# Page loads ahead of the mask, and one threshold search for blocks 4 to 7, in a hybrid decoder layer

## The chip, the cores and the metric

The kernel runs on one core of a Trainium2 chip. The metric is the device time of one execution in microseconds (us); lower is better. Engine names are those of the profile: PE (TensorE, with PEld for its weight loads), DVE (VectorE), ACT (ScalarE), POOL (GpSimd) and SP (SyncE, which here only issues transfers). An engine name with a q (SPq, DVEq) is that engine's sequencer.

## What is computed

One layer of a hybrid decoder for 1024 prompt tokens and, with the same weights, 64 sample tokens (8 sequences of 8, each with a cache of 4096 keys in 32 pages):

```python
x += 0.5 * swiglu(rms_norm(x), w1)
z  = rms_norm(x) @ w_in
#    attention: 8 query heads, 2 kv heads, dim 64, rotary; a token indexer picks the keys:
score = sum_h w[t,h] * relu(q_idx[t,h] . k_idx[s])
keep the 256 admissible keys of the largest score, softmax attention over these alone
#    short gated convolution, width 3: y = B * conv(C * h)
x += concat(attn, conv) @ w_out
x += 0.5 * swiglu(rms_norm(x), w2)
x += sigmoid(rms_norm(x) @ w_ple_gate) * (p @ w_ple_proj)
y  = rms_norm(x)
```

## The kernel before

**Tokens and products.** Tokens lie in columns, features in partitions. Group 0 has 576 columns, the 64 sample tokens and the prompt's blocks 0 to 3 (a block is 128 tokens), in two chunks of 288 (c0, c1). Group 1 is chunk c2 of 512 columns, blocks 4 to 7. A weight tile is 128 x 1024 in fp32. It is loaded raw (`load`, L603 to L610), ACT writes its rounded part (`w_hi`, `d_hi`, L834) and POOL the rest (`w_lo`, `d_lo`, L734), and each product is three matrix passes, hi by hi, lo by hi, hi by lo (L1442 to L1444). There are two raw buffers: a load waits until POOL has written the lo part two loads back, so SP, which issues the loads in order, sets the pace when it is held up.

**The order.** Class `Plan` writes one list of events (`order`, from L231), and each engine walks that list and does its own part of each event. The main line is a list of products, cut into parts. `weave(first, side, a, b)` hangs groups of side events on the places ("spots") between those parts, evenly from spot a to spot b. So an engine that is late with one event is late with all that the list has behind it, and a wait in one engine's program holds everything behind it on that engine.

**The stages**, in time: the norm of group 0 (`sq`, `sums`, `spread`, `scale`); SwiGLU 1 for group 0, with the gathering of indexer pages; the in-projection with the indexer's scores; SwiGLU 1 and the down products of c2, into which the sample tokens' search for their threshold is woven; the attention of the sample tokens and then of blocks 0 to 3, woven into the same products; `mix` and the out-projection of group 0; the in-projection of group 1; SwiGLU 2, into which the searches and the attention of blocks 4 to 7 are woven; out-projection, SwiGLU 2 of c2, embedding, final norm.

**Threshold search.** The 256th largest score of a row is found bit by bit. One iteration for two blocks (`bt`, `threshold_bit`, L1245 to L1259) is on DVE alone: a count per block of the scores at or above the candidate (L1242), a drain, a small operation per block (L1255), a drain, another per block (L1258), a drain. 32 iterations give the threshold. `places_left` (event `room`, L1264) and `choose` (event `bties`, L1274 to L1282) then settle equal scores and turn the score into a mask. Search A is for blocks 2 and 3, B1 for 4 and 5, B2 for 6 and 7. B1 has 8 iterations in the in-projection of group 1 and 24 in SwiGLU 2 ahead of the attention of block 4. B2's 32 iterations hang on the attention units of blocks 4 and 5,. The sample tokens have a like search of 32 bits over 2056 keys (`st`, L1284 to L1304), 12 in the in-projection and 20 behind it, then three events for ties (`sties`, L1308 to L1336), the last of which writes the mask `smask` (L1333) and lets go of semaphore `smask_ready`.

**Sample attention.** Behind the mask come: `sample_queries` on POOL (L766 to L778), the loads of pages of keys and values on SP (`kv_load`, L680 to L692; event kl), the split of the keys into `K_hi` on ACT (L993) and `kv_kr` on POOL (L784; event ks), the products of keys and queries on PE (event kq; L1442 to L1444 with `qs_hi`), the mask product (L1682) and the evacuation on DVE (`Sa`, L1384), then softmax, transposes and the product with the values (L1711). Buffers: 3 for keys, 8 for values.

```python
def kv_load(k):
    if k == 0:
        sp.wait_ge(smask_ready, 1)
```

Before every fourth kv_load, SP reads 16 page numbers from the table into registers (`page_numbers`, L613): one load and, for each number, a check of its bounds.

**Norm and mix.** `scale` multiplies x by the spread reciprocal (L1075), `spread` is a diagonal (L1069) times ones on PE (L1549). `mix` makes the hi and lo parts of the concatenated attention and convolution of a group: ACT writes four tiles of conv and then four of attn in two operations (L1020, L1021), POOL the lo part of conv (L788), DVE that of attn (L1425), and the out-projection waits for both.

Of the kernel before, what the change touches and what calls it, by code (L numbers as in the profile page):

```python
# [6 lines left out]
fp16 = mybir.dt.float16  # L7
# [36 lines left out]
SEARCH = {"A": (2, 3), "B1": (4, 5), "B2": (6, 7)}  # L44
EARLY = 8
# [50 lines left out]
class Plan:  # L96
# [134 lines left out]
    def order(self):  # L231
        squares = lambda k, c: [[("sq", k, c, m)] for m in range(KT)]
        flat = lambda groups: [e for g in groups for e in g]
        ev = [("begin",)] + flat(squares(0, 0)) + [("weights",)] + self.norm(0, 0) + flat(squares(0, 1)) + self.norm(0, 1)

        first = self.two_chunks(0, range(FT))
        first = weave(first, [[("ga", i)] for i in range(NB * PAGES // 2)], 1, 140)
# [13 lines left out]
        side += [[("st", j)] for j in range(12)]  # L251
# [3 lines left out]
        search = [[("st", j)] for j in range(12, 32)] + [[("sties", i)] for i in range(3)] + [[("qs",)]]  # L255
        groups = self.samples()
        for j in range(32):
            groups[6 + 2 * j].append(("bt", "A", j))
# [4 lines left out]
        first = weave(first, groups + units + [[], [("mix", 0)], [("back", 0)]], 51, -3)  # L263
        ev += weave(first, search, 2, 50)
# [6 lines left out]
        side += [[("bt", "B1", j)] for j in range(EARLY // 2)] + [[("vtr", 1)]] + [[("bt", "B1", j)] for j in range(EARLY // 2, EARLY)]  # L271
# [23 lines left out]
        ev += first[:end] + [("sums", 4, 0)] + first[end:end + 1] + [("spread", 4, 0)] + first[end + 1:]  # L295
# [3 lines left out]
    def with_weights(self, events):  # L299
# [9 lines left out]
        for e in events:  # L309
            if e[0] == "weights":  # L310
                for w in range(RING):
                    split(("w", w), "w", w)
# [77 lines left out]
def program(nc, t_in, t_out, x_spill, idx_flat):  # L390
# [5 lines left out]
    with ctx:  # L396
# [22 lines left out]
        small, small_i = at("small", [128, 64], f32, 5824), at("small_i", [128, 9], i32, 6080)  # L419
        carry = small[:, 0:8].rearrange("p (a b) -> p a b", b=2)  # L420
        mxr, nb, rs, ri = [small[:, 8 + 2 * j:10 + 2 * j] for j in range(4)]
        mx2, cnt, reached, room = small[:, 24:28].rearrange("p (a b) -> p a b", b=2), small[:, 28:36], small[:, 36:38], small[:, 38:40]
# [5 lines left out]
        cand, drop = [small_i[:, 2 * j:2 * j + 2] for j in range(2)]  # L428
# [169 lines left out]
        def _(sp):  # L598
# [81 lines left out]
            def kv_load(k):  # L680
                if k == 0:
                    sp.wait_ge(smask_ready, 1)
# [1129 lines left out]
```

## Time and profile before

| | us |
|---|---|
| median of 3 runs | 2928.32 |
| lowest and highest of them | 2918.21, 2932.49 |
| the profiled execution | 2924.44 |
| its span in the trace | 2922.7 |
| PE busy | 2615.3 (89% of the span) |
| DVE busy | 1313.0 (45%) |
| POOL busy | 1009.9 (35%) |
| ACT busy | 1001.1 (34%) |

The granted TensorE clock averages 0.943 of full speed over the profiled execution. Busy shares are averages over stages that have different limits; so the stages have to be read one by one. Drains and other sequencer work are not counted as busy.

### The profile page before, as it was taken

What the parts mean: (1) busy time and instruction counts of PE and PEld (TensorE: products, weight loads), DVE (VectorE), ACT (ScalarE), POOL (GpSimd) and SP (SyncE); (2) the same over time, 40 slices, a digit from 0 to 9 for tenths busy, and PEclk for the clock granted to TensorE, in tenths of its full rate; (3) what the DMA queues carried; (4) which work ended last, traced back from release to release, by engine and by line L of the source; (5) the groups of instructions that cost most, each with busy time, mean ns of one, the idle gap of its engine ahead of it and who ended that gap; (6) DMA issues with size and microseconds to landing.
All of it is one profiled execution on the core that took longest, in us unless ns stands there. A gap on an engine that the chain in (4) does not pass through costs nothing.

```text
span 2922.7 us, 41456 instructions
## 1 busy us (share of the span) xinstructions
PE 2615.3 (89%) x15166; PEld 2282.7 (78%) x15166; DVE 1313.0 (45%) x3135; ACT 1001.1 (34%) x1625; POOL 1009.9 (35%) x521
## 2 busy tenths in 40 slices
PE   4999998998868888889898976888999999999997
PEld 4999997778646767777786676777889898778786
DVE  3223224438753333443365687766333232332344
ACT  3222223631213333335435311443444233332332
POOL 4333333232343333332244223212213344454440
PEclk9999998999878888899999988998999999999998
DMA  4333324221224343311222212111112223233212
GB/s 147 98 95 100 107 92 140 93 106 63 96 79 124 103 136 116 119 57 49 77 101 75 70 61 73 44 44 44 44 44 87 80 72 115 87 108 96 92 63 73
DMA packets 157038, 253.40 MB, mean 87 GB/s; under 512 B 15010, under 2 KB 101283, under 8 KB 156835
## 3 DMA queue, kind: packets, MB, share of 16 engines
q1 hardware_dynamic: 154144, 247.02, 26.5%
q10 hardware_dynamic: 2690, 3.72, 0.4%
q8 instruction: 121, 1.98, 0.3%
q14 instruction: 83, 0.67, 0.1%
HBM read 240.34 MB, written 18.73 MB: 89 GB/s over the span
## 4 chain that ended last, share of the span: by engine, by line
PE 69%; DVE 14%; ACT 4%; issue 4%; POOL 3%; DVEq 2%; DMA 1%; SPq 1%; ACTq 0%
PE ps L1442 21%; PE ps L1443 19%; PE ps L1444 19%; PE ps L1655 2%; PE ps L1711 2%; DVE hits L1242 1%; POOL w_lo L734 1%; DVE s_hits L1292 1%; DVE hits_late L1242 1%; PE ps L1641 1%; DVE ps L1092 1%; POOL d_lo L734 1%; PE ps L1577 1%; DVE ha_lo L1094 1%; SPq L613 1%
## 5 line engine op out<-in xcount | busy, mean ns | idle before, releaser
L734 POOL TENSOR_TENSOR w_lo<-raw,w_hi 128x1024 fp32r<-128x1024 f32 x250 | 602.5, 2412 | 1058.7 <-ACT w_hi L834 1058.1
L1442 PE MATMUL ps<-xna_hi,w_hi 128*128 128x288 f32 x2000 | 612.3, 306 | 29.6 <-DVE convf_a L1146 7.8
L1443 PE MATMUL ps<-xna_lo,w_hi 128*128 128x288 f32 x2000 | 600.7, 300 | 0.0
L1444 PE MATMUL ps<-xna_hi,w_lo 128*128 128x288 f32 x2000 | 599.8, 300 | 0.0
L1442 PEld LDWEIGHTS ps<-xna_hi,w_hi 128*128 128x128 f32 x2000 | 387.6, 194 | 44.6 <-issue 22.8
L1442 PE MATMUL ps<-xnb_hi,w_hi 128*128 128x512 f32 x1000 | 412.8, 413 | 0.3 <-DVE hb_lo L1094 0.3
L734 POOL TENSOR_TENSOR d_lo<-raw,d_hi 128x1024 fp32r<-128x1024 f32 x90 | 218.4, 2446 | 544.6 <-ACT d_hi L834 544.6
L1443 PE MATMUL ps<-xnb_lo,w_hi 128*128 128x512 f32 x1000 | 400.6, 401 | 0.0
L1444 PE MATMUL ps<-xnb_hi,w_lo 128*128 128x512 f32 x1000 | 400.2, 400 | 0.0
L1443 PEld LDWEIGHTS ps<-xna_lo,w_hi 128*128 128x128 f32 x2000 | 387.3, 194 | 0.2
L1444 PEld LDWEIGHTS ps<-xna_hi,w_lo 128*128 128x128 f32 x2000 | 386.5, 193 | 0.0
L834 ACT ACTIVATE w_hi<-raw 128x1024 fp32r<-128x1024 f32 x250 | 263.6, 1055 | 193.0 <-PE ps L1444 106.1
L1442 PE MATMUL ps<-ha_hi,d_hi 128*128 128x288 f32 x704 | 216.2, 307 | 32.5 <-DVE xa L1183 28.8
L1442 PEld LDWEIGHTS ps<-xnb_hi,w_hi 128*128 128x128 f32 x1000 | 194.6, 195 | 46.1 <-issue 8.3
L1444 PEld LDWEIGHTS ps<-xnb_hi,w_lo 128*128 128x128 f32 x1000 | 194.3, 194 | 42.8
L1443 PEld LDWEIGHTS ps<-xnb_lo,w_hi 128*128 128x128 f32 x1000 | 194.8, 195 | 36.4
L1443 PE MATMUL ps<-ha_lo,d_hi 128*128 128x288 f32 x704 | 208.8, 297 | 0.0
L1444 PE MATMUL ps<-ha_hi,d_lo 128*128 128x288 f32 x704 | 208.4, 296 | 0.0
L834 ACT ACTIVATE d_hi<-raw 128x1024 fp32r<-128x1024 f32 x90 | 90.9, 1052 | 342.4 <-PE ps L1444 313.5
L1183 DVE SCALAR_TENSOR_TENSOR xa<-ps,xa 128x288 f32<-128x288 f32 x352 | 156.5, 455 | 109.7 <-PE ps L1444 109.4
L1183 DVE SCALAR_TENSOR_TENSOR xb<-ps,xb 128x512 f32<-128x512 f32 x176 | 121.6, 691 | 164.8 <-PE ps L1444 164.3
L1092 DVE TENSOR_TENSOR ps<-silu_a,ps 128x288 f32<-128x288 f32 x88 | 40.6, 462 | 287.0 <-PE ps L1444 274.8
(291 smaller groups left out, 4126.8 us busy)
## 6 DMA issues: line engine op xcount, KB each, us to landing
raw<-in_w_gu SPq DMA_DIRECT2D x176, 512.0 KB, 3.5
raw<-in_w_d SPq DMA_DIRECT2D x88, 512.0 KB, 3.5
raw<-in_w_ring SPq DMA_DIRECT2D x74, 512.0 KB, 3.4
pages<-in_vk_pages SPq DMA_DIRECT2D x256, 128.0 KB, 2.7
idx_flat<-in_idx_pages SPq DMA_DIRECT2D x256, 32.0 KB, 2.1
idxp<-idx_flat SPq DMA_DIRECT2D x8, 1024.0 KB, 7.6
x_spill<-xa SPq DMA_DIRECT2D x1, 2304.0 KB, 8.9
xa<-x_spill SPq DMA_DIRECT2D x4, 576.0 KB, 5.9
```

Of the source, the lines that this page charges most:

```text
L613: return nc.values_load_multi_w_load_instructions(ptab[0:1, first:first + k], engines=(mybir.EngineType.SP,), min_val=0, max_val=NPOOL - 1)[1]
L734: g_.tensor_tensor(lo[slot][:, :, :], raw[l % 2][:, :, :], hi[slot][:, :, :].bitcast(f32), ALU.subtract).then_inc(lo_done, 1)
L834: A(hi[slot][:, :, :], raw[l % 2][:, :, :], ACT.Copy).then_inc(hi_done, 1)
L1092: v.tensor_tensor(z, silu[g][:, own(c)], z, ALU.mult).then_inc(hmul_done, 1)
L1094: v.tensor_tensor(h_lo[g][h_at(c, j % 2)], z, h_hi[g][h_at(c, j % 2)].bitcast(f32), ALU.subtract).then_inc(h_ready, 1)
L1183: v.scalar_tensor_tensor(out=x[g][:, m, own(c)], in0=ps[:, 3 + (i - 1) % 2, 0:CH[c][1]], scalar=0.5, in1=x[g][:, m, own(c)], op0=ALU.mult, ...
L1242: v.tensor_scalar(hit[b][:, :], sc(b), level[:, i:i + 1], None, op, ALU.add, accum_out=reached[:, i:i + 1])
L1442: mm(out, shi, mhi, start=first, stop=False)
L1443: mm(out, shi, mlo, start=False, stop=False)
L1444: return mm(out, slo, mhi, start=False, stop=last)
L1655: mm(ps[rows, 7, c0:c0 + 128], V[:, j, rows], PT[g][r % 2][:, j, :], start=j == 0, stop=j == b)
L1711: last = mm(ps[:, 7, 64 * b:64 * b + 64], kv_v[(4 * ch + i) % V_RING][:, b, 128 * j:128 * j + 128], PTs[s][:, j, 64 * b:64 * b + 64], star ...
```

## The change

1. **Start.** The squares of the second chunk are woven into the norm of the first. Weight tiles 0 and 1 are split ahead of that norm as before, tiles 2 and 3 behind it. Product 0, on c0, starts ahead of the norm of c1.
2. **Sample search.** 10 of its 32 bits are in the in-projection, where 12 were; the other 22 and the ties are woven over spots 2 to 54 (2 to 50 before).
3. **Page loads and queries.** The first three kv_loads hang on the search's groups 2, 4 and 6 behind the in-projection, the first split of keys and `sample_queries` on its group 10. Their wait for the mask is replaced by a wait for the last product of the in-projection. For this, the key buffers `kv_kr`, `Sa`, the mask's and search's scratch lie elsewhere. The sample attention and blocks 0 to 3 go over spots 55 to -2 (51 to -3 before).
4. **Page numbers.** The check of bounds at run time is left out (`page_numbers`).
5. **Search B.** Blocks 4 to 7 have one search, 32 iterations of four counts, 8 of them in the in-projection of group 1 and 24 ahead of the attention of block 4. `bties` 5, 6 and 7 hang on the attention units 5, 10 and 15.
6. **Mix** goes tile by tile: ACT writes an attn tile and a conv tile in turn, DVE and POOL follow tile by tile, and the out-projection waits per tile.
7. **End.** `spread` of the last norm's c0 is behind the last embedding product, not one part ahead of it.

```diff
-SEARCH = {"A": (2, 3), "B1": (4, 5), "B2": (6, 7)}
+SEARCH = {"A": (2, 3), "B": (4, 5, 6, 7)}
...
-        ev = [("begin",)] + flat(squares(0, 0)) + [("weights",)] + self.norm(0, 0) + flat(squares(0, 1)) + self.norm(0, 1)
+        scales = lambda k, c, ms: [("scale", k, c, m) for m in ms]
+        second = flat(squares(0, 1))
+        ev = [("begin",)] + flat(squares(0, 0)) + [("weights", 0), ("sums", 0, 0)] + second[:4] + [("spread", 0, 0)]
+        ev += scales(0, 0, range(4)) + second[4:] + scales(0, 0, range(4, KT)) + [("weights", 1)]
...
+        ev += first[:1] + [("sums", 0, 1)] + first[1:2] + [("spread", 0, 1)] + scales(0, 1, range(KT))
...
-        side += [[("st", j)] for j in range(12)]
+        side += [[("st", j)] for j in range(10)]
...
-        search = [[("st", j)] for j in range(12, 32)] + [[("sties", i)] for i in range(3)] + [[("qs",)]]
+        search = [[("st", j)] for j in range(10, 32)] + [[("sties", i)] for i in range(3)]
         groups = self.samples()
+        for i in range(K_RING):
+            search[2 + 2 * i] += groups[i]
+        search[10] += [("qs",)] + groups[K_RING]
+        groups = groups[K_RING + 1:]
...
-        first = weave(first, groups + units + [[], [("mix", 0)], [("back", 0)]], 51, -3)
-        ev += weave(first, search, 2, 50)
+        first = weave(first, groups + units + [[], [("mix", 0)], [("back", 0)]], 55, -2)
+        ev += weave(first, search, 2, 54)
...
-        side = [[("bt", "B1", j)] for j in range(EARLY, 32)] + [[("room", "B1")]] + [[("bties", b)] for b in SEARCH["B1"]]
-        late = [[("bt", "B2", j)] for j in range(32)] + [[("room", "B2"), ("bties", 6)]] + [[("bties", 7)]]
-        for i, g in enumerate(units):
-            side.append((late[i] if i < len(late) else []) + g)
+        side = [[("bt", "B", j)] for j in range(EARLY, 32)] + [[("room", "B")]] + [[("bties", 4)]]
+        for b in (5, 6, 7):
+            units[5 * (b - 4)].append(("bties", b))
+        side += units
...
-        ev += first[:end] + [("sums", 4, 0)] + first[end:end + 1] + [("spread", 4, 0)] + first[end + 1:]
+        ev += first[:end] + [("sums", 4, 0)] + first[end:] + [("spread", 4, 0)]
...
-                                                                min_val=0, max_val=NPOOL - 1)[1]
+                                                                min_val=0, max_val=NPOOL - 1,
+                                                                skip_runtime_bounds_check_because="a page table holds pages of the pool")[1]
...
                 if k == 0:
-                    sp.wait_ge(smask_ready, 1)
+                    sp.wait_ge(prod_done, last_in[0] + 1)
...
-                pool.wait_ge(mix_hi, 2 * g + 1)
-                g_.tensor_tensor(xn_lo[g][:, 4:8, :], convf[g][:, :, :], xn_hi[g][:, 4:8, :].bitcast(f32), ALU.subtract).then_inc(mixc_ready, 1)
+                for j in range(4):
+                    pool.wait_ge(mix_hi, 8 * g + 2 * j + 2)
+                    g_.tensor_tensor(xn_lo[g][:, 4 + j, :], convf[g][:, j, :], xn_hi[g][:, 4 + j, :].bitcast(f32), ALU.subtract).then_inc(mixc_ready, 1)
...
-                A(xn_hi[g][:, 4:8, :], convf[g][:, :, :], ACT.Copy).then_inc(mix_hi, 1)
-                A(xn_hi[g][:, 0:4, :], attn[g][:, :, :], ACT.Copy).then_inc(mix_hi, 1)
+                for j in range(4):
+                    A(xn_hi[g][:, j, :], attn[g][:, j, :], ACT.Copy).then_inc(mix_hi, 1)
+                    A(xn_hi[g][:, 4 + j, :], convf[g][:, j, :], ACT.Copy).then_inc(mix_hi, 1)
...
-                for i in range(2):
+                for i in range(len(blocks)):
                     v.tensor_scalar(drop[:, i:i + 1], reached[:, i:i + 1], TOPK - 0.5, float(2 ** (31 - j)) if j else -1.0, ALU.is_lt, ALU.mult)
```

**Order of DVE at the end of the search, ahead of the first attention of block 4.** Scores 131 to 134 are those of blocks 4 to 7; L1102, L1104 and L1193 of the new file are the old L1092, L1094 and L1183 (work on the main products). Before:

```order
L1242 TENSOR_SCALAR hits_late,small<-score_131,small_i 128x640
L1242 TENSOR_SCALAR hits_late,small<-score_132,small_i 128x768
L1264 TENSOR_SCALAR small<-small 128x2
L1092 TENSOR_TENSOR ps<-silu_a,ps 128x288
L1094 TENSOR_TENSOR ha_lo<-ps,ha_hi 128x288
L1183 SCALAR_TENSOR_TENSOR xa<-ps,xa 128x288 x8
L1274 TENSOR_SCALAR equal_b<-score_131,small_i 128x640
```

In the changed kernel, the same place:

```order
L1252 TENSOR_SCALAR hits_late,small<-score_131,small_i 128x640
L1252 TENSOR_SCALAR hits_late,small<-score_132,small_i 128x768
L1252 TENSOR_SCALAR hits_late,small<-score_133,small_i 128x896
L1252 TENSOR_SCALAR hits_late,small<-score_134,small_i 128x1024
L1274 TENSOR_SCALAR small<-small 128x4
L1284 TENSOR_SCALAR equal_b<-score_131,small_i 128x640
```

The two larger counts now stand in every iteration ahead of the attention; before, they stood behind it, between attention units of blocks 4 and 5.

**Order of POOL around the sample queries.** Before (L767 to L778 are `sample_queries`):

```order
L734 TENSOR_TENSOR d_lo_76<-raw_64,d_hi_74 128x1024
L767 MEMSET qs_f 128x768
L773 COPY qs_f<-attn_a 64x4x8 x16
L776 CAST qs_hi<-qs_f 128x768
L778 TENSOR_TENSOR qs_lo<-qs_f,qs_hi 128x768
L734 TENSOR_TENSOR w_lo_71<-raw_63,w_hi_67 128x1024
L734 TENSOR_TENSOR w_lo_72<-raw_64,w_hi_68 128x1024
L784 TENSOR_TENSOR kv_kr_192<-pages,K_hi_123 128x512
L784 TENSOR_TENSOR kv_kr_193<-pages,K_hi_124 128x512
```

In the changed kernel:

```order
L744 TENSOR_TENSOR w_lo_71<-raw_63,w_hi_67 128x1024
L777 MEMSET qs_f 128x768
L783 COPY qs_f<-attn_a 64x4x8 x16
L786 CAST qs_hi<-qs_f 128x768
L788 TENSOR_TENSOR qs_lo<-qs_f,qs_hi 128x768
L794 TENSOR_TENSOR kv_kr_194<-pages,K_hi_123 128x512
L744 TENSOR_TENSOR w_lo_72<-raw_64,w_hi_68 128x1024
```

The queries and the first split of keys are a dozen weight splits ahead of the second split of keys, that is, in the midst of the search.

**Order of SP around the first page loads.** Before (L613 reads the page numbers, L692 is a page load):

```order
L610 DMA raw_63<-in_w_gu 128x1024
L613 TENSOR_LOAD ptab
L613 ISA x32
L692 ISA
L692 DMA pages<-in_vk_pages 128x2x128
```

In the changed kernel:

```order
L619 DMA raw_64<-in_w_d 128x1024
L622 TENSOR_LOAD ptab
L702 ISA
L702 DMA pages<-in_vk_pages 128x2x128
```

The 32 instructions of the bounds check are gone, and the first page load stands some 50 weight-load rows earlier in SP's program.

## Rows read from the trace of the kernel before

**Rows 1.** The page, busy time of each engine.

```profile
PE 2615.3 (89%) x15166; PEld 2282.7 (78%) x15166; DVE 1313.0 (45%) x3135; ACT 1001.1 (34%) x1625; POOL 1009.9 (35%) x521
```

**Rows 2.** Windows: stretch, us, PE, PEld, DVE, ACT, POOL busy, PEclk, DMA share, GB/s.

```profile
640.00:851.00 211.00, 179.55 (x897) 155.02 (x896) 175.48 (x327) 46.11 (x60) 89.07 (x44) 0.91 0.23 75
851.00:872.00 21.00, 1.43 (x7) 1.06 (x6) 0.05 (x1) 2.55 (x5) 10.18 (x15) 0.63 0.27 82
872.00:1294.00 422.00, 363.55 (x1847) 301.61 (x1846) 155.67 (x559) 141.74 (x232) 145.10 (x91) 0.85 0.38 111
1294.00:1447.00 153.00, 143.67 (x737) 107.12 (x736) 61.67 (x201) 79.98 (x167) 40.30 (x20) 0.99 0.16 52
1690.00:1812.00 122.00, 93.52 (x646) 91.61 (x644) 95.05 (x260) 22.25 (x34) 36.49 (x15) 0.90 0.21 66
1812.00:2050.00 238.00, 200.53 (x1293) 179.16 (x1293) 166.89 (x482) 96.07 (x156) 50.19 (x23) 0.91 0.14 45
2050.00:2245.00 195.00, 190.81 (x1342) 170.60 (x1342) 62.19 (x191) 92.33 (x140) 44.10 (x19) 1.00 0.15 49
```

**Rows 3.** Timeline of the start, ACT and PE: start, us, engine, instruction [idle before].

```profile
20.34 1.06 ACT L834 ACTIVATE w_hi<-raw 128x1024 fp32r<-128x1024 f32 x1 [5.73 <-DMA raw<-in_w_gu]
22.99 1.28 ACT L860 ACT_TABLE_LOAD   x1
41.75 0.59 PE L1442 MATMUL ps<-xna_hi,w_hi 128*128 128x288 f32 x1
```

**Rows 4.** Timeline behind the mask: DVE, POOL, SP, ACT, PE.

```profile
847.85 0.69 DVE L1333 TENSOR_SCALAR smask<-above 128x2056 bf16<-128x2056 bf16 x1
853.83 1.80 POOL L778 TENSOR_TENSOR qs_lo<-qs_f,qs_hi 128x768 fp32r<-128x768 f32 x1
863.61 4.69 SPq L692 DMA_DIRECT2D pages<-in_vk_pages  x6
868.86 0.63 ACT L993 ACTIVATE K_hi<-pages 128x512 fp32r<-128x512 f32 x1 [16.16 <-DMA pages<-in_vk_pages]
870.97 0.55 PE L1442 MATMUL ps<-K_hi,qs_hi 128*128 128x256 f32 x1 [19.57 <-POOL kv_kr L784]
```

**Rows 5.** Line 613 on SP, 858 to 864 us: count, ns min/median/max, first and last start.

```profile
L613 SPq FUSED_REGOPS  x16: 147/147/165, 859.4 to 863.2; - x16
```

**Rows 6.** Waits of PE: 872 to 1294 us, then 1812 to 2050: us, times, longest.

```profile
PE ps L1442 <- POOL kv_kr L784: 44.7, 15, 4.7
...
PE ps L1442 <- DVE small L1347: 21.8, 11, 6.6
```

**Rows 7.** Timeline of DVE: an iteration of B1, then one of B2.

```profile
1673.95 0.88 DVE L1242 TENSOR_SCALAR_CACHE_REDUCE hits_early<-score,small_i 128x640 bf16<-128x640 f32 x1 [0.16 <-issue]
1676.57 0.88 DVE L1242 TENSOR_SCALAR_CACHE_REDUCE hits_early<-score,small_i 128x640 bf16<-128x640 f32 x1
...
1814.12 1.15 DVE L1242 TENSOR_SCALAR_CACHE_REDUCE hits<-score,small_i 128x896 bf16<-128x896 f32 x1
1816.55 0.21 DVE L1255 TENSOR_SCALAR small_i<-small 128x1 int32<-128x1 f32 x2
1816.84 0.34 DVE L1258 TENSOR_SCALAR small_i<-small_i 128x1 int32<-128x1 int32 x2
```

**Rows 8.** Timeline of DVE: the ties of block 5, first and last operation.

```profile
1801.55 0.61 DVE L1274 TENSOR_SCALAR equal_b<-score,small_i 128x768 bf16<-128x768 f32 x1
1810.15 0.56 DVE L1282 TENSOR_SCALAR score<-score 128x768 f32<-128x768 f32 x1
```

**Rows 9.** Timeline of the mix of group 0: POOL, DVE, PE.

```profile
1445.88 5.07 POOL L788 TENSOR_TENSOR xna_lo<-convf_a,xna_hi 128x2304 fp32r<-128x2304 f32 x1
1447.49 5.87 DVE L1425 TENSOR_TENSOR xna_lo<-attn_a,xna_hi 128x2304 fp32r<-128x2304 f32 x1 [7.98 <-ACT xna_hi L1021]
1453.62 0.58 PE L1442 MATMUL ps<-xna_hi,w_hi 128*128 128x288 f32 x1 [6.34 <-DVE xna_lo L1425]
```

**Rows 10.** Timeline of DVE near the end: the last norm's scales.

```profile
2909.61 3.48 DVE L1075 SCALAR_TENSOR_TENSOR xna_f<-xa,consts,ps 128x288 f32<-128x288 f32 x8
```

More of the change, by code:

```diff
@@ L310, in with_weights @@
             if e[0] == "weights":
-                for w in range(RING):
+                for w in (2 * e[1], 2 * e[1] + 1):
                     split(("w", w), "w", w)
@@ L427, in program @@
         s_w, s_f = small[:, 28:32], small[:, 32:36]
-        cand, drop = [small_i[:, 2 * j:2 * j + 2] for j in range(2)]
-        s_cand, s_with_bit, s_drop = [small_i[:, 6 + j:7 + j] for j in range(3)]
+        room = {"A": small[:, 40:42], "B": small[:, 28:32]}
+        cand, drop = [small_i[:, 4 * j:4 * j + 4] for j in range(2)]
+        s_cand, s_with_bit, s_drop = [small_i[:, 8 + j:9 + j] for j in range(3)]
         raw = [at(f"raw{s}", [128, KT, 128], f32, 38912 + 4096 * s) for s in range(2)]
@@ L499, in program @@
         inv = [at("inv_a", [128, 128], f32, XNA + 16384), at("inv_b", [128, 128], f32, XNB + 24576)]
-        above = at("above", [128, HW], bf16, XNA + 17152)
-        cum = at("cum", [128, HW], fp16, XNA + 21280)
-        Sa = [at(f"Sa{s}", [128, 1024 + NS], f32, XNA + 16384 + 4352 * s) for s in range(2)]
+        above = at("above", [128, HW], bf16, XNA + 6144)
+        cum = at("cum", [128, HW], fp16, XNA + 10272)
+        Sa = [at(f"Sa{s}", [128, 1024 + NS * s], f32, FREE + 4096 * s) for s in range(2)]
         qs_hi, qs_lo, qs_f = [at(name, [128, 4, 192], dt, XNA + o) for name, dt, o in (("qs_hi", f32r, 25088), ("qs_lo", f32r, 28160), ("qs_f", f32, 28160))]
@@ L1277, in choose @@
                 dve.drain()
-                v.scalar_tensor_tensor(out=ti, in0=ti, scalar=room[:, i:i + 1], in1=e, op0=ALU.is_gt, op1=ALU.mult)
+                v.scalar_tensor_tensor(out=ti, in0=ti, scalar=room[name][:, i:i + 1], in1=e, op0=ALU.is_gt, op1=ALU.mult)
                 dve.drain()
@@ L1423, in mix @@
             def mix(g):
-                dve.wait_ge(mix_hi, 2 * g + 2)
-                v.tensor_tensor(xn_lo[g][:, 0:4, :], attn[g][:, :, :], xn_hi[g][:, 0:4, :].bitcast(f32), ALU.subtract).then_inc(mixa_ready, 1)
+                for j in range(4):
+                    dve.wait_ge(mix_hi, 8 * g + 2 * j + 1)
+                    v.tensor_tensor(xn_lo[g][:, j, :], attn[g][:, j, :], xn_hi[g][:, j, :].bitcast(f32), ALU.subtract).then_inc(mixa_ready, 1)
             does = {"begin": begin, "sq": square, "sums": sums, "spread": spread, "scale": scale, "p": product, "d": add,
@@ L1496, in product @@
                         pe.wait_ge(lo_done, plan.pos["w", w] + 1)
-                    if kind == "out" and key[0] == 0:
-                        pe.wait_ge(mixa_ready, g + 1)
-                        pe.wait_ge(mixc_ready, g + 1)
                 k = {"gate": 2 * key[0], "up": 2 * key[0], "in": 1, "out": None, "pg": 3}[kind]
@@ L1505, in product @@
                         normed(k, c, kt)
+                    elif (g, kt) not in mixed:
+                        mixed.add((g, kt))
+                        pe.wait_ge(*((mixa_ready, 4 * g + kt + 1) if kt < 4 else (mixc_ready, 4 * g + kt - 3)))
                     last = split_mm(out, hi[slot][:, kt, :], lo[slot][:, kt, :], xn_hi[g][:, kt, own(c)], xn_lo[g][:, kt, own(c)], kt == 0, kt == KT - 1)
```

52 lines of the change are left out of this document (25 added, 27 removed).

## The prediction

> **What bounds the kernel now.** I read the page's busy times first, then a table of windows by stage, then the timelines of the gaps. PE is busy for 2615 us of 2923 [rows 1], so over the whole program the products bound it, and only the stretches in which PE idles or has a low clock can give anything. The windows [rows 2] show three kinds. From 2050 to 2245 PE is busy 190.8 of 195 us at full clock: nothing to gain. From 640 to 851 (sample search) and from 1690 to 1812 (search B1) DVE sets the pace: its busy time is 175 of 211 and 95 of 122 us, and drains and dispatch, which are not counted, fill the rest. From 872 to 1294 (sample attention) no engine is full, but PE idles 58 us in short waits, and the granted clock is 0.85, which is another 63 us (15% of 422) below full speed. Between them stands a hole: from 851 to 872 PE works 1.4 us.
>
> **Start.** PE's first product pass is at 41.75 [rows 3]. ACT must split tiles 2 and 3 before it may compute the first norm, and idles 5.7 us for their load: from about 14.6, where tiles 0 and 1 are done, to 22.99, where the table load for the norm starts, 8.4 us go by. The change lets the norm go first, and runs product 0 on c0 before c1 is normed. Upper bound of the gain: 8.4 plus part of one chunk's product (24 passes, which start 0.24 us apart in the same timeline, 5.8 us), limited by weights that then are needed sooner: 12. Lower: 6, if the fourth tile's split becomes the next wait. **I take -10.**
>
> **Mask to first sample product.** The mask is written at 847.85 to 848.54. Only then POOL builds the queries, until 855.6, SP reads page numbers and issues page loads from 863.61 on, ACT splits the first keys at 868.86, and PE starts at 870.97 after 19.57 us of waiting [rows 4]. Afterwards all of this lies in the search. POOL's 6.7 us there (848.9 to 855.6) cost nothing, since POOL is busy 89 of 211 us and PE waits for DVE [rows 2]. On SP three kv_loads of four page DMAs at 4.69/6 = 0.78 us, 3.1 us each, plus the first read of numbers, are moved past weight loads; the DVE-bound search covers them. If that cover were gone, each could hold a weight load by 3 to 4 us, 12 in all. What stays: two more iterations and the ties behind the in-projection end the search some 3.5 us later, the mask product and its evacuation take about 2, and PE has about one more product part to do meanwhile. First sample product at 854 to 855: **-16.5**, between -12 and -20.
>
> **Sample attention.** SP reads 16 numbers before every fourth kv_load, and checks each: 16 checks start between 859.4 and 863.2, 0.253 us apart [rows 5], so 4.05 us of each read goes. PE waits 44.7 us in 15 waits for the keys' lo part, the longest 4.7 [rows 6]. But POOL, which makes it, is also in the queue behind weight splits, and only about five of these waits, some 15 us together, lie where SP was reading numbers. The others stay. From these I take 11 us. The first three key blocks are loaded ahead, so the wait and the low clock of the first 28 us go too: the first passes at 870.97 take 0.55 us against 0.41 of the next [rows 4], at the 0.63 clock of the hole [rows 2]; I put 8. And 3 for clock regained behind shorter waits. **-22**; nothing if POOL's queue is what sets these waits, -35 if nearly all go. The units are also spread a little tighter (117 groups on 99 spots, where 121 were on 102): nothing.
>
> After a wait the trace shows the clock low: 0.63 in the hole, 0.85 over the waits of this stage, 1.00 where PE hardly idles [rows 2]. The Trainium skill, page "TensorE: Matmul & The Clock Gate", section "HAM oscillation — how this bites in real kernels", says that a wait that comes back in every round of a loop drops TensorE to half clock each round, so that it costs more than its own length. The rows agree; by this rule the five shorter waits would give more than the 3 us that I add, which is the way of the second rival below.
>
> **Page reads elsewhere.** The gathers of the first stage get shorter by about 2 us per read of 8; loads run ahead there. Nothing.
>
> **Mix.** DVE's lo part of attn takes 5.87 us, 1447.49 to 1453.36, while POOL's of conv runs until 1450.95; it seems to run in its last 2.4 us alone. PE idles 6.34 us for it, to 1453.62 [rows 9]. By tiles the out-projection starts at about 1447 and follows the tiles, whose last comes at 1451 to 1453.5. Its own 5.8 us of passes then overlap. **-4**, between -2 and -7. The Trainium skill, page "SBUF — State Buffer", section "Who interferes with whom", says that a DVE operation with two SBUF inputs and a GpSimd operation exclude each other for a whole instruction. The row looks just like this; by the rule smaller operations do not overlap either, and the gain is 5 and not 6.
>
> **Search B.** An iteration of B1 takes 1676.57 - 1673.95 = 2.62 us. The two larger counts with their drain take 1816.55 - 1814.12 = 2.43, 2.27 without the drain, and two more of each small operation (0.21 and 0.34 for two, started 0.29 and some 0.43 apart) about 0.4 [rows 7]. So an iteration of four is 2.62 + 2.27 + 0.4 = 5.29, 2.67 more; 32 of them put 85.4 us on DVE ahead of the first attention unit of block 4. To this comes the larger `room`, 2.3. Off this path go the ties of block 5, 1801.55 to 1810.71, 9.2 us [rows 8], and the first four B2 iterations that DVE ran before the first logits, 12.6; and DVE has about 4 us of slack in the in-projection. 85.4 + 2.3 - 9.2 - 12.6 - 4 = 62; with a little for waits of PE behind longer iterations **+64**. None of this is covered: DVE is the bound there [rows 2], and PE's products wait behind it (its banks of PSUM are emptied by DVE).
>
> What comes back: from 1812 to 2050 DVE had 28 iterations of 3.15 us between its logits, and PE idled 37 us and lost 0.09 of 238, 21 us, to the clock [rows 2]; 21.8 of the idle were waits for logits evacuated late [rows 6]. Without the search the stretch should look like its neighbours. At the 98% of 2050 to 2245 it would give 45 us beyond what is counted above; at the 94% of 1294 to 1447 (blocks 2 and 3, no search) 35. The ties of blocks 5, 6 and 7 now stand in it (9, 6 and 7 us without logits), which costs about 5. **-30**; bounds -45 and, if the attention's own chain of logits, exponent and transposes sets these waits, -10. Search B in all: +34, from +19 to +54.
>
> **End.** The diagonal, spread and eight scales (3.48 us, [rows 10]) of the last norm come behind the last part instead of beside it: **+2**, from 0 to +3.
>
> **Sum.** -10 - 16.5 - 22 - 4 + 64 - 30 + 2 = -16.5 us. The profiled execution took 2924.4, 3.9 below the median, so it gives 2907.9 there and about **2911 us** against the median of 2928.3. About 0.5% (14.6 us) is what a measurement of this kernel can tell from no change: faster is below 2913.7, slower above 2942.9.
>
> **Rivals.**
> 1. *The search isn't paid back, slower.* Place: DVE, 1690 on. The other parts make -10 - 16.5 - 4 + 2 = -28.5, the search +64: +35.5 stands before sample attention and recovery, which together must give over 35.5 for any gain. If the short waits in the sample attention are POOL's queue (0 to -2) and the attention of blocks 4 to 7 is held by its own chain (-8), the kernel takes 2924.4 + 26 = 2950, or 2954 on the median's scale. For it: DVE is the only engine at its limit from 1690 to 1812, and every one of the 85 us lands there. Against it: the stretch from 2050 on shows what attention without a search does, at larger blocks. It decides from a recovery under about 16 us with no gain in the sample attention.
> 2. *Large gain.* Recovery 45, sample attention 35: 35.5 - 80 = -44.5, 2880, or 2884 against the median. For it: 98% and a full clock from 2050 on; the clock comes back with the idle. Against it: POOL's place in the chain of the keys, and the ties.
> 3. *The hole only shrinks.* The new loads don't do what they should: PE reaches the mask product early and now waits there for DVE, which has two more iterations and the evacuation, or weights are late behind the page loads. Mask to product -5, sample attention -12: the sum is +5, 2929.4, or 2933. For it: DVE, not the loads, sets when the mask comes, and it comes later. Against it: the chain from 848.5 to 871 has no work of DVE in it [rows 4].
>
> **Chances.** The forecast 0.42, its own range 2895 to 2927, of which some two thirds lie below 2913.7; rival 1 0.19; rival 2 0.21; rival 3 0.18, mostly within 0.5%. Faster: 0.28 + 0.21 = 0.49; same: 0.14 + 0.16 + 0.03 = 0.33; slower: 0.16 + 0.02 = 0.18. The range takes in most of rival 2 and half of rival 1: 2880 to 2950.
>
> **What would show it.** In the changed profile: first product pass at 30 to 33 us; PE's gap before the first pass on K_hi under 4 us, and L1384 within 3 us of the mask; no FUSED_REGOPS on the line of the page numbers, 11 us less of PE's waits for kv_kr, a clock over 0.87 in the sample attention; a first out-projection pass on the mixed input within 2 us of the last product; iterations of four counts every 5.3 us, the stretch from the first late one to the ties of block 4 about 62 us longer; PE busy 94% or more from there to the out-projection, and few waits for logits. I am wrong if iterations are shorter than 4.9 us, if DVE has other slack that hides them, or if the waits of PE in the attention stay as they were without the search on DVE.

## The result, and the profile after

The changed kernel takes **2934.91 us** (median of 20 runs, 2920.82 to 2941.59) against 2925.6 us for the kernel before (20 runs, 2918.21 to 2934.79): ratio 1.0026, 95% interval 1.0014 to 1.0038. That is slower by 0.26%, within the 0.5% that I called no change. I had forecast 2911, with a range of its own from 2895 to 2927, and a 0.33 chance of no change. The profiled execution took 2941.6 us and is the slowest of the 20, 6.7 above their median; keep that in mind with the offsets below, which come from this execution.

Windows of the changed kernel, by the same stages as [rows 2] (columns as there):

```profile
650.00:837.00 187.00, 164.25 (x795) 139.29 (x793) 147.27 (x299) 41.42 (x51) 78.98 (x49) 0.94 0.28 88
837.00:847.00 10.00, 1.03 (x5) 0.69 (x4) 8.88 (x6) 0.00 (x0) 8.15 (x3) 0.77 0.32 106
847.00:1250.00 403.00, 351.88 (x1821) 292.47 (x1821) 158.47 (x553) 140.09 (x231) 140.25 (x89) 0.87 0.39 114
1615.00:1668.00 53.00, 38.59 (x180) 32.06 (x178) 49.93 (x146) 9.62 (x11) 14.31 (x6) 0.88 0.17 50
1668.00:1833.00 165.00, 85.81 (x512) 83.55 (x513) 140.93 (x432) 17.70 (x28) 28.49 (x12) 0.72 0.13 42
1833.00:2060.00 227.00, 209.50 (x1398) 190.51 (x1397) 90.54 (x241) 99.29 (x158) 56.37 (x25) 0.94 0.16 52
2060.00:2258.00 198.00, 193.55 (x1363) 173.03 (x1362) 63.21 (x195) 94.27 (x145) 44.10 (x19) 1.00 0.15 48
```

The hole of 21 us is 10 now, the sample attention is at clock 0.87 and not 0.85. In their place stands the row from 1668 to 1833: 165 us in which PE is busy for half and its clock averages 0.72. Behind it (1833 on) PE is at 92%.

The two traces can be laid over each other, since PE runs the same 12312 passes on weights, numbered from 0, in the same order. This table, worked out from both traces, gives how much later (+) the changed kernel starts the same pass:

| pass number | where | changed minus before, us |
|---|---|---|
| 0 | first product | -18.8 |
| 400 to 3200 | SwiGLU 1, in-projection | -13.7 |
| 3600 | late in-projection | -18.7 |
| 4400 | in the sample search | -14.1 |
| 4800 | in the sample attention | -33.9 |
| 5600 | blocks 2, 3 | -40.8 |
| 6400 | in-projection of group 1 | -40.6 |
| 6800 | late joint search begun | -6.5 |
| 7200 | its end | +41.2 |
| 8000 | attention of group 1 | +22.9 |
| 9200 to 11200 | to the embedding | +10.7 to +12.2 |
| 12311 | last | +14.7 |

Everything ahead of search B gains 40 us; search B takes 82, and 29 come back behind it. Such offsets scatter from one execution to the next. Experiments 1, 3, 5 and 12 run the changed kernel's order up to pass 6400, and their offsets to the kernel before stand there at -52.0, -45.9, -41.4 and -41.3, where the changed kernel has -40.6.

The rows that answer to [rows 3], [rows 4], DVE, PE, in the changed kernel:

```profile
14.72 1.28 ACT L871 ACT_TABLE_LOAD   x1
...
22.91 0.58 PE L1453 MATMUL ps<-xna_hi,w_hi 128*128 128x288 f32 x1 [2.04 <-POOL xna_lo L750]
...
845.24 0.70 DVE L1343 TENSOR_SCALAR smask<-above 128x2056 bf16<-128x2056 bf16 x1
848.32 0.42 DVE L1394 TENSOR_SCALAR_CACHE_REDUCE Sa<-ps 128x256 f32<-128x256 f32 x1 [2.11 <-PE ps L1693]
...
846.34 0.55 PE L1453 MATMUL ps<-K_hi,qs_hi 128*128 128x256 f32 x1 [8.97 <-issue]
```

The table load is 8.3 us earlier, as said. The first sample product follows the mask at once: keys and queries are ready. But PE has waited 8.97 us for the mask, since its program waits for it ahead of the key products (L1675 of the new file) and not ahead of the mask product (L1693), which is the first to read it.

Two joint iterations that follow each other on DVE (answer to [rows 7]):

```profile
1750.04 0.87 DVE L1252 TENSOR_SCALAR_CACHE_REDUCE hits_late<-score,small_i 128x640 bf16<-128x640 f32 x1
...
1755.28 0.88 DVE L1252 TENSOR_SCALAR_CACHE_REDUCE hits_late<-score,small_i 128x640 bf16<-128x640 f32 x1
```

5.24 us, where I had 5.29. The unit price was right; the waits around it were not. Waits of DVE from the first joint iteration to the first logits (us, times, longest), of the changed kernel:

```profile
DVE xa L1193 <- PE ps L1455: 18.1, 24, 1.5
DVE ps L1102 <- PE ps L1455: 6.0, 1, 6.0
DVE ha_lo L1104 <- ACT ha_hi L895: 5.8, 10, 1.5
```

and of the kernel before, over its stretch from the first B1 iteration:

```profile
DVE xa L1183 <- PE ps L1444: 13.0, 24, 1.5
DVE ha_lo L1094 <- ACT ha_hi L884: 4.8, 10, 0.5
DVE ps L1092 <- PE ps L1444: 2.3, 2, 1.4
DVE tb L1151 <- PE ps L1444: 1.9, 2, 1.5
```

The sum of these waits went up by about 8 us (22.0 to 29.9), where I had counted 4 us of slack to be used up. Of the 29.9 us, 13.0 lie behind the last joint iteration, in the 23 us before the first logits.

### The profile page after: what moved, and what is told of

Same layout as the page of the kernel before. It is cut to its first block, busy times and chain, and to the rows that moved or that the text cites. A ratio compares the mean times of both kernels' runs of the same rounds, so it can differ in the third digit from the quotient of the medians.

```text
span 2939.8 us, 40350 instructions
## 1 busy us (share of the span) xinstructions
PE 2622.8 (89%) x15166; PEld 2290.8 (78%) x15166; DVE 1303.8 (44%) x3139; ACT 1001.0 (34%) x1637; POOL 1010.7 (34%) x527
## 4 chain that ended last, share of the span: by engine, by line
PE 71%; DVE 15%; ACT 4%; issue 3%; POOL 3%; DVEq 1%; DMA 1%; ACTq 0%; SPq 0%
PE ps L1453 21%; PE ps L1454 20%; PE ps L1455 20%; DVE hits_late L1252 3%; PE ps L1666 2%; PE ps L1722 2%; PE ps L1652 1%; POOL w_lo L744 1%; DVE s_hits L1302 1%; POOL d_lo L744 1%; DVE hits_early L1252 1%; DVE ps L1102 1%; PE ps L1588 1%; ACT w_hi L845 1%; DVE ha_lo L1104 1%
## 5 line engine op out<-in xcount | busy, mean ns | idle before, releaser
L1193 DVE SCALAR_TENSOR_TENSOR xa<-ps,xa 128x288 f32<-128x288 f32 x352 | 156.4, 455 | 117.6 <-PE ps L1455 117.4
L1453 PEld LDWEIGHTS ps<-ha_hi,d_hi 128*128 128x128 f32 x704 | 137.7, 196 | 85.4 <-DVE xa L1193 64.4
L1193 DVE SCALAR_TENSOR_TENSOR xb<-ps,xb 128x512 f32<-128x512 f32 x176 | 121.4, 691 | 173.9 <-PE ps L1455 173.4
```

The lines of the kernel that those rows point to most:

```text
L1193: v.scalar_tensor_tensor(out=x[g][:, m, own(c)], in0=ps[:, 3 + (i - 1) % 2, 0:CH[c][1]], scalar=0.5, in1=x[g][:, m, own(c)], op0=ALU.mult, ...
L1453: mm(out, shi, mhi, start=first, stop=False)
```

## The experiments

All were run in several rounds beside the kernel before on the same chip; experiments 1 to 4, 5 to 8 and 9 to 12 ran on three different chips. "Against the changed kernel" below is a difference of two such ratios, times 2926; each ratio is uncertain by about 0.0015 to 0.002, so such a difference by some 6 us, and by 8 between experiments 1 and 9.

**1. The change without the joint search.** Part 5 put back, all else as changed.

```diff
-SEARCH = {"A": (2, 3), "B": (4, 5, 6, 7)}
+SEARCH = {"A": (2, 3), "B1": (4, 5), "B2": (6, 7)}
...
+        late = [[("bt", "B2", j)] for j in range(32)] + [[("room", "B2"), ("bties", 6)]] + [[("bties", 7)]]
```

> The changed kernel with only its part 5 (one search for blocks 4 to 7) put back as before: B1 of 24 iterations ahead of the attention, B2 inside it. Theory (the joint search costs about 53 us net, which is what the offset between the two traces grows by from the in-projection of group 1 to the out-projection): 2935 - 53 = 2882 us, ratio to the kernel before about 0.985. Rival 1 (it costs the 34 us of the prediction, and the other parts gave less than forecast): 2901 us, ratio 0.992. Rival 2 (the search is neutral, the rest gave nothing): 2935.

2885.62 us, ratio 0.9858 (0.9839 to 0.9877). Against the changed kernel -49 us. The theory stands, its rivals fall. The offset of its passes to the kernel before is -52 us when group 1's in-projection starts, and stays at -50 to -54 to the embedding. The prediction had summed -52.5 for the parts ahead of that point (-10 - 16.5 - 22 - 4), but that the two agree is luck: this profiled execution is at the fast end of its runs, some 9 us below their median, so the median's share is nearer to -43, and the changed kernel's own trace has -40.6 there. From that point on the two traces differ by 54 us.

**2. The joint search alone.** Part 5 in the kernel before.

```diff
-SEARCH = {"A": (2, 3), "B1": (4, 5), "B2": (6, 7)}
+SEARCH = {"A": (2, 3), "B": (4, 5, 6, 7)}
```

> The kernel before with only part 5 of the change. Theory: 2926 + 53 = 2979 us, ratio 1.018. Rival 1 (34 us): 2960, ratio 1.012. If both this and the split search give 53 the parts add up; if this gives much less, the joint search hurts only in company of the other parts.

2970.22 us, ratio 1.0147 (1.0124 to 1.017): +43 us. In its trace the search adds 79 us and the attention gives 33 back. The loss is the joint search's own; 43 lies in the middle between 53 and 34, and by the two pairs the joint search costs 43 to 49 us, which are one number within the error.

**3. Eight iterations fewer.**

```diff
-        side = [[("bt", "B", j)] for j in range(EARLY, 32)] + [[("room", "B")]] + [[("bties", 4)]]
+        side = [[("bt", "B", j)] if j < 24 else [] for j in range(EARLY, 32)] + [[("room", "B")]] + [[("bties", 4)]]
```

> The changed kernel with the last 8 of the 24 late joint iterations left out (so the thresholds of blocks 4 to 7 lack their 8 lowest bits), their spots kept empty. If DVE alone sets the pace there, 8 x 5.29 = 42 us go: 2893. If, as I now suspect, DVE's waits for PE grow with the low clock of PE between the iterations (8.7 us more such waits in the changed trace over 24 + 8 iterations, where the forecast had 4 us less), an iteration is worth 5.7 to 6 us: 2888. If PE, not DVE, set the pace, under 30 us go: over 2905.

2896.53 us, ratio 0.9883 (0.9866 to 0.9901): 42 us below the changed kernel. By the offset of the passes only 34 of it lie in the search; 5 lie in stages ahead, which this edit does not touch, and so are scatter. Windows of the stretch with iterations, and of the empty one behind it:

```profile
1663.00:1769.00 106.00, 55.69 (x323) 54.21 (x324) 90.18 (x273) 11.57 (x18) 17.40 (x8) 0.71 0.11 36
1769.00:1795.00 26.00, 25.65 (x193) 25.42 (x193) 11.03 (x31) 6.25 (x10) 11.16 (x5) 1.00 0.39 123
```

Where the iterations are gone, PE is busy 25.65 of 26 us at full clock, and it, not DVE, sets the pace. Eight iterations of 5.24 us are 42 us; 34 came, and the rest is what PE needs for its own products there. My guess of 5.7 to 6 us an iteration is not borne out; nor is the rival in which PE sets the pace throughout (under 30 us).

**4. The check of page numbers put back** into the changed kernel.

```diff
-                                                                min_val=0, max_val=NPOOL - 1,
-                                                                skip_runtime_bounds_check_because="a page table holds pages of the pool")[1]
+                                                                min_val=0, max_val=NPOOL - 1)[1]
```

> The changed kernel with the run-time check of the page numbers put back (4.05 us more per read of 16 numbers, 16 reads). Theory (five or so waits of PE lie behind a read, and the clock falls with them): +14 us, 2949, ratio 1.008. Rival (POOL's queue of weight splits sets the waits for the keys' lo part, the reads are hidden): 0 to +3, 2935 to 2938. Third: the first read now stands inside the search, so nothing there.

2964.7 us, ratio 1.0127 (1.0108 to 1.0145): +30 us, twice the theory, and the two rivals (0 to +3, nothing) fall. The profiled pair differs by 21.8 us, and by the passes 20.5 of it arise between the first sample product and the out-projection. PE's waits of that stage, with the check,

```profile
PE ps L1452 <- POOL kv_kr L793: 52.5, 20, 5.1
```

and in the changed kernel,

```profile
PE ps L1453 <- POOL kv_kr L794: 42.8, 15, 4.7
```

are 10 us apart. The clock is 0.84, against 0.87 in the changed kernel:

```profile
849.00:1272.00 423.00, 359.99 (x1801) 297.47 (x1801) 154.78 (x551) 138.17 (x228) 139.57 (x88) 0.84 0.38 109
```

PE is busy for 8 us more than in the changed kernel's row (847 to 1250), on 20 fewer operations; that is the part of the clock.

**5. PE kept busy in the search.**

```diff
+            def warm(name, j):
+                if name == "B" and j >= EARLY:
+                    for _ in range(5):
+                        mm(ps[:, 6, 0:128], ones[:, :], ident[:, 0, :], start=True, stop=True)
```

> The changed kernel with five idle matrix products (ones times identity, 128 columns, into a PSUM bank that nobody reads, about 0.5 us each) on PE at each of the 24 late joint iterations. Theory: DVE's waits for PE in the search (18.1 + 7.6 + 5.8 us on the adds and the SwiGLU products, against 13.0 + 3.4 + 4.8 before) grow because PE comes out of each wait at half clock; with PE kept busy its clock stays up, these waits fall back by up to 10 us, and the kernel takes 2925 to 2930. Rival: they are the latency of a product that DVE has asked for late, whatever the clock; then 2935, or slower by as much as the idle products delay a real one (up to 2950).

2933.48 us, ratio 1.0015 (1.0002 to 1.0028): 3 us less than the changed kernel, within the error; the theory's 5 to 10 us did not come.

```profile
1668.00:1833.00 165.00, 104.87 (x737) 103.15 (x737) 142.10 (x435) 17.70 (x28) 28.42 (x12) 0.79 0.14 42
```

PE's clock rose from 0.72 to 0.79, DVE's waits on the additions fell from 18.1 to 15.8 us, and the search ended about as late as before (1 to 2 us). So 0.07 of clock gives back a small part of the waits. The experiment did not bring the clock to 1.00, so it doesn't exclude that the clock explains more of them. The rest is taken to be the time of a product part that PE can start only when DVE has emptied a bank; that was not tried by itself.

**6. Pages and queries behind the mask again.**

```diff
-        for i in range(K_RING):
-            search[2 + 2 * i] += groups[i]
-        search[10] += [("qs",)] + groups[K_RING]
-        groups = groups[K_RING + 1:]
...
-                    sp.wait_ge(prod_done, last_in[0] + 1)
+                    sp.wait_ge(smask_ready, 1)
...
-                pool.wait_ge(prod_done, last_in[0] + 1)
+                pool.wait_ge(smask_ready, 1)
```

> The changed kernel with its part 3 undone: sample queries, first page loads and first split of keys wait for the mask again and stand behind it (memory map and all else as changed). Theory: the hole of 21 us comes back in place of the 9 us that PE now waits for the mask, and the clock falls with it: +11 to +17, 2946 to 2952, ratio 1.0065 to 1.0085. Rival: the early loads hold up the weight loads in the search, or set back the key ring, so that they gain little: 2935 to 2940.

2946.69 us, ratio 1.0049 (1.0031 to 1.0066): +7 us, between the theory (+11 to +17) and the rival (0 to +5), and not to be told from either within the error. The first sample product starts at 858.8 and not 846.3, 12.5 us later, and PE waits 20.0 us there and not 9.0. But fewer products are done at that moment in the changed kernel (at pass 4800 the kernel of this run is even 9 us ahead, at pass 6000 9 us behind). The edit also puts 121 groups, not 117, on the same 99 spots, and the mask is written at 840.2 and not 845.2, since the search's last group hangs on an earlier spot. So part of the 7 us can be these, and the early loads are not weighed cleanly.

**7. Mix in its old form.**

```diff
-                for j in range(4):
-                    A(xn_hi[g][:, j, :], attn[g][:, j, :], ACT.Copy).then_inc(mix_hi, 1)
-                    A(xn_hi[g][:, 4 + j, :], convf[g][:, j, :], ACT.Copy).then_inc(mix_hi, 1)
+                A(xn_hi[g][:, 4:8, :], convf[g][:, :, :], ACT.Copy).then_inc(mix_hi, 1)
+                A(xn_hi[g][:, 0:4, :], attn[g][:, :, :], ACT.Copy).then_inc(mix_hi, 1)
...
```

> The changed kernel with mix in its old form (part 6 undone). Prediction on record: +4. Theory from the changed trace (the four DVE and four POOL operations alternate and take 9.4 us together where two long ones took 7.5; PE starts at once but waits for each tile): 0 to +2, 2935 to 2937. Rival: +6, 2941.

2937.33 us, ratio 1.0023 (1.001 to 1.0036): no difference. In the changed kernel:

```profile
1406.70 7.60 POOL L799 TENSOR_TENSOR xna_lo<-convf_a,xna_hi 128x576 fp32r<-128x576 f32 x4
...
1404.85 8.17 DVE L1436 TENSOR_TENSOR xna_lo<-attn_a,xna_hi 128x576 fp32r<-128x576 f32 x4 [3.13 <-ACT xna_hi L1030]
```

Four tiles each take 7.60 and 8.17 us side by side, 9.45 from the first start to the last end; the two long operations took 7.48 [rows 9]. They take turns: DVE's tiles start at 1404.85, 1407.27, 1409.19 and 1411.07, POOL's at 1406.70, 1408.61, 1410.49 and 1412.37. By the Trainium skill, page "SBUF — State Buffer", section "Who interferes with whom", such a pair excludes each other for a whole instruction. These rows agree.

PE does idle less at this place: 0.80 + 1.21 + 1.21 us in the changed kernel, 6.20 us in one wait with the old form. By the passes of the two traces the tiles bring the first mixed pass 6.4 us forward; 3.4 are left once the last tile is there, and 1.9 twenty passes later. The 1.5 us between are clock: at passes 5736 to 5741 PE is still at the low clock in the changed kernel, 0.43 us from one pass of 512 columns to the next, where with the old form it is 0.23. In the next in-projection 0.7 are left; where the rest went the record doesn't show, and such amounts are within the scatter.

**8. The check left out, alone.** The edit of experiment 4 the other way, in the kernel before. It takes out 512 checks, 256 in 16 reads of 16 numbers and 256 in 32 reads of 8 for the gathers.

> The kernel before with part 4 alone (no run-time check of page numbers). Theory (as when the check is put back into the changed kernel, +30 us): 2926 - 25 = 2901, and in the windows most of it between 872 and 1294 us, half as clock and half as idle. Rival: in the order before, the reads lie elsewhere; -14 us as predicted for the five waits and their clock, 2912. The waits for the keys' lo part alone can't tell, they sum to 43 to 46 us in all kernels but that with the check in the changed order (52.7).

2902.4 us, ratio 0.9912 (0.9896 to 0.9929): -26 us. The theory stands; its rival, the 14 us of the prediction, falls. By the passes 20 us of it lie in the hole and the sample attention (4 ahead of the first sample product, 16 behind it), and 4 between passes 100 and 200: the first read of numbers for the gathers had held up the weight loads behind it on SP, and a wait of PE of 2.9 us at 65 us is gone.

**9. Split searches, 12 bits, old end.** Experiment 1 with 12 bits of the sample search in the in-projection, and the last spread where it was.

```diff
-        side += [[("st", j)] for j in range(10)]
+        side += [[("st", j)] for j in range(12)]
...
-        search = [[("st", j)] for j in range(10, 32)] + [[("sties", i)] for i in range(3)]
+        search = [[("st", j)] for j in range(12, 32)] + [[("sties", i)] for i in range(3)]
...
-        ev += first[:end] + [("sums", 4, 0)] + first[end:] + [("spread", 4, 0)]
+        ev += first[:end] + [("sums", 4, 0)] + first[end:end + 1] + [("spread", 4, 0)] + first[end + 1:]
```

> The changed kernel with the searches of blocks 4 to 7 split as before, 12 and not 10 bits of the sample search in the in-projection, and the last norm's spread where it was. Against the run with the split searches alone (2885.6): the two bits cost 2 x 3.5 us of DVE in the search and gave 5 to 9 in the in-projection, so -2 to +3, and the end -2: 2880 to 2886. Rival: the search's place decides by more (the mask comes 7 us earlier and the K blocks are there): 2876.

**2876.18 us**, ratio 0.9824 (0.9804 to 0.9844), the fastest of the kernels that compute the whole layer: 10 us below experiment 1, where the error is about 8. It agrees with the rival's number, 2876. At pass 3600, late in the in-projection, its trace is 7 us later than that of experiment 1, and from the sample attention on 5 us earlier; the mask is there at 839.1 and not 842.9. The two profiled executions differ by 4 us only, so the trace bears out the sign, and less than the 10 us. The two bits moved out of the in-projection cost more than I gave them.

**10. The same, sample attention two spots later.**

```diff
-        first = weave(first, groups + units + [[], [("mix", 0)], [("back", 0)]], 55, -2)
+        first = weave(first, groups + units + [[], [("mix", 0)], [("back", 0)]], 57, -2)
```

> As the first run of this call, with the sample attention starting two spots later (57), so that PE has products to do in the 9 us that it waits for the mask. Theory: -3 to -6, 2876 to 2880, if PE can run these products without DVE (three banks of PSUM). Rival: the products need DVE's additions, which stand behind the ties, so PE stops anyway: the same as the first, and a denser sample attention takes back a little: 2883 to 2890.

2889.35 us, ratio 0.9868 (0.9848 to 0.9888): 13 us slower. The number lies in the rival's range, but not for the rival's first reason: PE does not stop as long as before. It waits 5.4 and not 9.2 us for the mask, and is 12.6 us ahead at pass 4800. Then the sample attention, with 117 groups on 97 spots and not 99, loses 32 us by pass 6000, where the rival had "a little": its waits for the keys' lo part are 50.6 us and not 42.9, and its clock goes from 0.89 to 0.85. These two don't make up 32 us; the rest was not traced.

**11. The start alone**, in the kernel before (part 1's lines of the diff).

> The kernel before with part 1 alone (start). The prediction had -10; the changed trace shows products 13.7 us earlier from 60 us on, of which 4.0 could be the shorter first read of page numbers (products 4.0 us earlier there in the kernel with that edit alone). If they add up: -10, 2917. If the start itself gives all: -14, 2913.

2913.92 us, ratio 0.9954 (0.994 to 0.9969): -13 us, all of it there by pass 400 (-13.1 in its trace, -13.8 in the changed kernel's). The start gives this by itself; the 4 us that the shorter first read gave in experiment 8 don't come on top.

**12. Split searches without B2**: what the search inside the attention costs.

```diff
-        late = [[("bt", "B2", j)] for j in range(32)] + [[("room", "B2"), ("bties", 6)]] + [[("bties", 7)]]
+        late = [[("bt", "B2", 0)]] + [[] for j in range(1, 32)] + [[("room", "B2"), ("bties", 6)]] + [[("bties", 7)]]
```

> The changed kernel with split searches and 31 of the 32 iterations of B2 left out (blocks 6 and 7 get a threshold of one bit), their places in the attention of blocks 4 and 5 kept empty. It is the price of B2 inside the attention alone. By the prediction 12.6 ahead of the first logits and 35 to 45 in the attention, so -48 to -58: 2828 to 2838. By what the traces of the joint search show (20 to 33 us recovered, with 12.6 of it ahead of the first logits or more): -33 to -40, 2846 to 2853, and the attention stretch still idles behind its own chain.

2849.23 us, ratio 0.9735 (0.9716 to 0.9753): 36 us below experiment 1, as the second estimate said. 31 iterations of 3.15 us are 98 us of DVE time, and take only 36 of the kernel's, since PE has work beside most of them. Without them the attention of blocks 4 and 5 runs at 94%, nearly at full clock:

```profile
1771.00:1930.00 159.00, 150.03 (x1038) 135.61 (x1038) 57.94 (x184) 75.80 (x123) 41.79 (x19) 0.98 0.19 57
```

Ahead of the attention, the counts cost their full length: 32 iterations that are 2.62 us longer make 84 us, and the passes of the changed kernel fall back by 82.

## Why the prediction was wrong

Each part but the mix moved the kernel the way that was forecast, and their sum did not: 2911 was forecast, 2935 measured, outside the forecast's own range and within the wide one of 2880 to 2950. The step that failed most is Search B. Its cost was put at +64 and what comes back at -30; the profiled pair has +72.4 and -20, so two large terms of opposite sign were both sized in favour of the change. Next come the two bits of the sample search, whose cost ahead of the mask was put at 3.5 us, and the mix.

- **Start, -10:** measured -13 (experiment 11). The first product starts at 22.9, not at 30 to 33.
- **Mask to first sample product, -16.5:** the first sample product is 24.6 us earlier, of which 13.7 are the start's: -11. Of the 19.57 us of waiting 8.97 stay. The step that failed is the search's end "some 3.5 us later" for two more iterations and the ties: with the start's 13.7 us taken out, the mask is written 11 us later. The two iterations alone are 7 us, 3.48 each; the other 4 were not tried by themselves, but in experiment 6, where the search's last group hangs on an earlier spot, the mask comes 5 us earlier. And PE waits for the mask at the head of the key products. That is rival 3's mechanism, PE waiting for DVE's mask, and I had argued against it. Undoing the early loads cost 7 us in all (experiment 6).
- **Sample attention, -22:** from the first sample product to the out-projection the profiled pair gained 16 us, the pair with experiment 1 24, so the term is about right, but not for my reasons. The check alone is worth 16 to 20 us in this stretch (experiments 8 and 4), where I gave the reads 11 and 3 for clock, and 26 to 30 in the whole kernel. The waits for the keys' lo part were to fall by 11 us and went from 44.7 to 42.8. The 8 us for the wait and the clock of the first 28 us rest on a misreading: the passes of 0.41 us that I set against 0.55 are at the low clock too. They start 0.21 us apart, where over half of these passes in this stage start 0.12 us apart; and the first pass of the changed kernel takes 0.55 us as well.
- **Page reads elsewhere, nothing:** 4 us in the kernel before (experiment 8), nothing beside the new start (experiment 11).
- **Mix, -4:** 0 within the error (experiment 7). The step that failed is that a start ahead of the last tile is kept as time: DVE and POOL took turns for 9.45 us, so that the first mixed pass came 6.4 us earlier but the last tile did not, and of the 3.4 us that were gained by then 0.7 are left in the next in-projection.
- **Search B, +34:** measured +49 (experiment 1) and +43 (experiment 2), inside my bounds of 19 and 54, and the largest error. The profiled pairs have 52 to 54 and 46. Two steps failed. First, "about 4 us of slack": from the first joint iteration to the first logits DVE takes 241.3 us against 168.9, +72.4, where my terms give 62. The iteration was right (5.24). But DVE didn't find slack, it waited about 8 us more for PE and ACT. My reading is that with PE held up by DVE, and DVE then by PE's parts that start late, the two are partly in series; experiment 5 took back 2 us of these waits through the clock, and no run tried the buffers, so the cause of the 8 us stays open. Second, "what comes back, -30": the offset of the passes shrinks by 20 from the first logits on. PE at 94% without a search was foreseen rightly (experiment 12), and the changed kernel comes near it (92% from 1833 on). What was too large is what this gives: all of B2 is worth 36 us, ahead of the logits and in the attention together, where I had 12.6 + 35 to 45, less 5 for the ties.
- **End, +2:** not measured alone. From the start of the last weight pass to the end of the span it takes 15.3 us in the six traces with the old end, and 17.0 to 17.7 in the eight with the new one: 1.7 to 2.4 more. The spread's passes, which stood ahead of that point, give a part of it back, so this bears out a term between 0 and +2.
- **Not in the sum:** the two bits moved. Experiment 9 gains 10 us, uncertain by 8, from them and the end together, so about 8 for the bits, and by the traces 2 to 5.

Sum of what was measured: start -13, check -30, early pages -7, joint search +49, bits and end +10, mix 0 = +9; the two medians differ by 9.3. That this is so close is luck, since each term is uncertain by 4 to 8 us; with the check and the joint search as measured in the kernel before (-26, +43) the sum is +7.

None of the rivals came true as it stood. Rival 1 needed a recovery under about 16 us and no gain in the sample attention; the recovery was 20 and the gain 16 to 24. Rival 3's mechanism was seen (8.97 us of waiting for the mask), at about half its size; that its 2933 lies next to the 2935 measured is luck, since the search cost 9 to 15 us more than it assumed and the check gave more. Without the check's 26 to 30 us the change would have been slower by over 1% (experiment 4).

## What to carry to other kernels

Work put on DVE where DVE was the bound cost its full length here (82 of 84 us); counts of the same kind beside PE's work cost about a third of theirs (36 of 98 us). So before work is gathered "to have it done ahead", ask which engine bounds the place that it goes to. Look also at what a queue that only issues transfers does between them: 4 us of checks per read of page numbers were the largest single gain in this change. And where two engines wait for each other in turn, don't count slack on one side as cover before a trace shows it: here 4 us were counted, and 8 us of waits were added.

## What was not expected of the hardware

- 512 checks of 0.253 us on SP, 130 us in 48 reads, were worth 26 us of the kernel alone and 30 in company, part of it as clock (the granted clock of the sample attention rose from 0.85 to 0.87 in experiment 8).
- Two spots fewer for 117 groups lost 32 us in the sample attention (experiment 10); its short waits for POOL grew by 8 us and its clock fell from 0.89 to 0.85.
- Products on PE whose result nobody reads raised its granted clock from 0.72 to 0.79 in a stretch in which DVE set the pace, and the time moved by 3 us, within the error (experiment 5).
